# Hybrid decoder step on one core: where v's negated absolute value stands, and how the gate rows are spread over the partitions

## What is computed

```python
proj = h @ w_in
qkv, z, a, b = split(proj)
qkv = silu(causal_conv(qkv, buf, conv_w))      # 4 taps; q, k, v of 128 features each
beta = sigmoid(b)
g = -exp(A_log) * softplus(a + dt_bias)        # one number per token and head
G = cumsum(g)                                  # within a chunk of 128 tokens
decay = exp(G[t] - G[s])
M = eye + strict_lower(beta * (k k^T) * decay)
u, w = M^-1 (v * beta), M^-1 (k * beta * exp(G))
v_new = u - w S;  o = q exp(G) S + (q k^T * decay) v_new
S = exp(G_last) S + (k exp(G_last - G))^T v_new
```

## Time and profile before

| | us |
|---|---|
| median of 3 runs | 1731.76 |
| lowest, highest | 1729.2, 1732.01 |
| the profiled execution | 1732.29 |
| its span, first to last instruction | 1730.5 |
| PE busy / DVE busy / ACT busy | 1664.7 / 1083.1 / 722.5 |
| mean granted TensorE clock | 0.982 of full speed |

### The profile page before, as it was taken

How to read it: one execution, slowest core, us unless ns; L and a number is a source line. 1 busy time by engine, 2 the same in 40 slices (tenths; PEclk the granted TensorE clock), 3 DMA queues, 4 the chain that set the end, 5 groups by cost and what they waited for, 6 DMA issues and landing times.

```text
span 1730.5 us, 33084 instructions
## 1 busy us (share of the span) xinstructions
PE 1664.7 (96%) x12561; PEld 1583.7 (92%) x12561; DVE 1083.1 (63%) x2126; ACT 722.5 (42%) x1315; POOL 35.8 (2%) x85
## 2 busy tenths in 40 slices
PE   6999999999999999999999999999999999999997
PEld 6999999899999999999888888888788999999997
DVE  6898889866435353457778778777846535343443
ACT  6565556534222121225456546655634212222233
POOL 0000000000000000000000000000000000000000
PEclk8999999999999999999999999999998999999998
DMA  6223222222322223222220221122122233222321
GB/s 177 62 83 89 81 81 86 75 74 85 96 86 86 86 86 94 86 74 74 64 64 27 76 64 51 37 67 72 53 62 76 88 93 90 86 85 86 91 79 52
DMA packets 257855, 135.17 MB, mean 78 GB/s; under 512 B 6746, under 2 KB 256180, under 8 KB 257780
## 3 DMA queue, kind: packets, MB, share of 16 engines
q1 hardware_dynamic: 220256, 114.53, 23.0%
q10 hardware_dynamic: 37524, 19.58, 3.9%
HBM read 122.09 MB, written 12.00 MB: 77 GB/s over the span
## 4 chain that ended last, share of the span: by engine, by line
PE 80%; DVE 10%; ACT 5%; issue 3%; ACTq 1%; DMA 0%; DVEq 0%
PE pj L520 66%; PE rr L558 3%; DVE pr L2014 2%; DVE w_lo L1660 1%; PE rr L541 1%; PE rr L633 1%; PE rr L679 1%; PE rr L821 1%; PE rr L837 1%; ACT w_hi L1060 1%; PE rr L748 1%; PE rr L911 1%; PE rr L801 1%; DMA pr<-in_gdn_conv_w_dram 0%; PE rr L917 0%
## 5 line engine op out<-in xcount | busy, mean ns | idle before, releaser
L520 PE MATMUL pj<-xh,w_hi 128*128 128x272 f32 x2064 | 455.7, 302 | 6.6 <-DVE xl L1684 4.7
L1060 ACT ACTIVATE w_hi<-w_raw 128x1024 fp32r<-128x1024 f32 x211 | 222.5, 1055 | 570.0 <-PE pj L520 552.0
L520 PE MATMUL pj<-xh,w_lo 128*128 128x272 f32 x2064 | 431.3, 291 | 0.0
L520 PE MATMUL pj<-xl,w_hi 128*128 128x272 f32 x2064 | 430.1, 290 | 0.0
L520 PEld LDWEIGHTS pj<-xh,w_hi 128*128 128x128 f32 x2064 | 327.0, 191 | 27.2 <-issue 19.6
L520 PEld LDWEIGHTS pj<-xl,w_hi 128*128 128x128 f32 x2064 | 328.7, 191 | 0.0
L520 PEld LDWEIGHTS pj<-xh,w_lo 128*128 128x128 f32 x2064 | 327.0, 191 | 0.0
L1660 DVE TENSOR_TENSOR w_lo<-w_raw,w_hi 128x1024 fp32r<-128x1024 f32 x211 | 256.8, 1217 | 34.0 <-ACT w_hi L1060 33.9
L520 PE MATMUL pj<-oh,w_hi 128*128 128x272 f32 x1254 | 266.7, 294 | 9.1 <-DVE w_lo L1660 6.4
L520 PE MATMUL pj<-oh,w_lo 128*128 128x272 f32 x1254 | 262.1, 291 | 0.0
L520 PE MATMUL pj<-ol,w_hi 128*128 128x272 f32 x1254 | 261.2, 290 | 0.0
(11 more groups left out here) (335 smaller groups left out, 1975.6 us busy)
## 6 DMA issues: line engine op xcount, KB each, us to landing
w_raw<-in_mlp_w_up_dram SPq DMA_DIRECT2D x64, 512.0 KB, 4.0
w_raw<-in_mlp_w_down_dram SPq DMA_DIRECT2D x64, 512.0 KB, 3.6
w_raw<-in_hgrn_w_in_dram SPq DMA_DIRECT2D x32, 512.0 KB, 4.0
w_raw<-in_gdn_w_in_dram SPq DMA_DIRECT2D x32, 512.0 KB, 4.1
out_dram<-S ACTq DMA_DIRECT2D x16, 512.0 KB, 3.2
S<-in_state_hgrn_dram ACTq DMA_DIRECT2D x8, 512.0 KB, 4.0
w_raw<-in_hgrn_w_out_dram SPq DMA_DIRECT2D x8, 512.0 KB, 3.7
S<-in_state_gdn_dram ACTq DMA_DIRECT2D x8, 512.0 KB, 4.1
```

The source lines that it names most:

```text
L520: last = mm(pj[:, s, b, 0:HALF], w[:, s, k, :], v[:, k, b * HALF:(b + 1) * HALF], start=(k == 0 and a == 0), stop=(k == end - 1 and a == 2))
L1060: f(w_hi[:, c % SPLIT, 0:n], w_raw[:, slot, 0:n], ACT.Copy).then_inc(w_high, 1)
```

## The change

It does three things.

- **vneg moves.** DVE makes -|v| of the next head no longer behind the v taps but behind the first chunk's state (L1781), ahead of silu of q; for that it becomes a slot of its own. ACT's slot L6 (exponential and logarithm of it) moves from level 64 to behind the copies of chunk 0, ahead of the square of q. In head 0's own preparation the order is as before.
- **The gate rows are rounded once.** After the gates are made, ACT rounds the lower 64 partitions of `gt4` to fp32r (step `high`, into `gate_parts[0:64]`), and DVE subtracts this from them and rounds the rest into the upper 64 (`low`). Per head DVE no longer makes the 128x544 product but a selector `head_rows` of 128x2 (constant columns, now repeated over the upper half, times the head's column), and PE multiplies `gate_parts` by a selector column in fp32r: one record a matmul where there were two. PE waits once for `low`.
- **gt4 moves** into an unused row of the work space.

```diff
--- before.py
+++ after.py
@@ -75,8 +75,8 @@
     same = s[:, None] // SLEN == s[None, :] // SLEN
     cf[:TS, C_INCLS:C_INCLS + TS] = same & (s[None, :] >= s[:, None])
     cf[:TS, C_NSTRS:C_NSTRS + TS] = -(same & (s[None, :] > s[:, None])).astype(np.float32)
-    cf[0:32, C_IND] = 1
-    cf[32:64, C_IND + 1] = 1
+    cf[:, C_IND] = p // 32 % 2 == 0
+    cf[:, C_IND + 1] = p // 32 % 2 == 1
     cf[:, C_HSEL:C_HSEL + H] = p[:, None] % 32 == np.arange(H)[None, :]
 
     cu = np.zeros((P, 2, len(LEVELS), T // 2), np.uint8)
@@ -159,7 +159,7 @@
         cu = sb("cu", [P, 2 * len(LEVELS) * (T // 2)], U8)
         vec = sb("vec", [P, V_N])
         cw = sb("cw", [P, CONV, 3 * H])
-        hc = sb("hc", [P, 16])
+        hc = sb("hc", [P, 6])
         lbt = sb("lbt", [P, 4, H])
         ones = sb("ones", [P, P])
         epsc = sb("epsc", [P, 2])
@@ -206,7 +206,9 @@
         Sp = sb("Sp", [P, NC, P])
         S0 = sb("S0", [P, NSEQ, P])
 
-        gt4 = sb("gt4", [P, T])
+        gt4 = gd["spare"]
+        gate_parts = sb("gate_parts", [P, T], F32R)
+        head_rows = sb("head_rows", [P, 2], F32R)
         gcol = sb("gcol", [P, NC + 1, 4 * H])
         gnext = sb("gnext", [P, NC + 1])
         gcols = sb("gcols", [P, NC + 1, 4])
@@ -257,10 +259,10 @@
             hr=["d2", "d4", "kl2", "adiag", "kd", "pred1", "d8", "kl4", "pred2", "d16", "kl8", "pred4", "qe",
                 "d32", "kl16", "pred8", "S0", "S1", "S2", "S3", "gate", "d64", "kl32", "pred16", "vbig", "sdec", "kl64", "pred32",
                 "snew", "pred64", "on", "og", "lo"],
-            gp=["x", "neg", "ls", "g", "g2", "scan", "dl", "turn"],
+            gp=["x", "neg", "ls", "g", "g2", "scan", "dl", "turn", "low"],
 
             ga=["cols", "gsel", "k1", "k2", "k3", "kneg", "kls", "q1", "q2", "q3", "qneg", "dec", "ks", "qls",
-                "v1", "v2", "v3", "vneg", "kn", "kb", "qs", "kkd", "vls", "vs", "qn", "zneg", "qkd", "nl", "tt0", "tt1",
+                "v1", "v2", "v3", "kn", "kb", "vneg", "qs", "kkd", "vls", "vs", "qn", "zneg", "qkd", "nl", "tt0", "tt1",
                 "A", "zls", "qe", "cols2", "nbe"],
             ga0=["hcw", "k1", "k2", "k3", "kneg", "cols", "gsel", "kls", "ks", "q1", "dec", "q2", "q3", "qneg", "kn", "kb", "qls", "qs",
                  "kkd", "v1", "v2", "v3", "vneg", "qn", "nl", "tt0", "tt1", "zneg", "qkd", "vls", "vs", "zls", "A",
@@ -279,7 +281,7 @@
             ha=["fabs", "fexp", "fln", "nabs", "cexp", "cln", "qabs", "qexp", "qln", "qsig", "K", "gabs", "gexp", "gln", "e1",
                 "gsig", "ebd"],
             hr=["e2", "e4", "vT", "kdT", "e8", "kdTs", "e16", "e32", "os", "e64", "sq", "oo", "ln", "rn", "hi"],
-            gp=["A", "exp", "ln", "be", "el", "eg", "cols"],
+            gp=["A", "exp", "ln", "be", "el", "high", "eg", "cols"],
             ga=["hist", "past", "ktap", "qtap", "vhist", "kexp", "kln", "G", "ksig", "qexp", "qln", "bb", "dec",
                 "sqk", "vtap", "qsig", "lnk", "rnk", "eG", "vexp", "vln", "sqq", "vsig", "lnq", "rnq", "zexp", "zln", "cout",
                 "K", "tm0", "zsig"],
@@ -725,8 +727,8 @@
                         pe.wait_ge(s.sem, s.after("G" if g else "hist", h))
                     pe.wait_ge(v.sem, v.after("gsel", h))
                     for b in range(2):
-                        last = mm(rr[:, (0 if own else 2) + b, 0:HALF], cf[:, C_IND + g:C_IND + g + 1].broadcast_to([P, P]),
-                                  work[:, b * HALF:(b + 1) * HALF], start=True, stop=True)
+                        last = mm(rr[:, (0 if own else 2) + b, 0:HALF], head_rows[:, g:g + 1].broadcast_to([P, P]),
+                                  gate_parts[:, b * HALF:(b + 1) * HALF], start=True, stop=True)
                     t.did(last, name)
                 if slot == "L5":
                     pe.wait_ge(s.sem, s.after("sqk", h))
@@ -979,6 +981,7 @@
             gdn_pre()
             more(5)
             pe.wait_ge(st["gp"][1].sem, st["gp"][1].after("cols", 0))
+            pe.wait_ge(st["gp"][0].sem, st["gp"][0].after("low", 0))
             gdn_prepare("L3", 0)
             gdn_prepare("L4", 0)
             more(4)
@@ -1268,6 +1271,8 @@
                     last = f(o, i, ACT.Exp)
                 s.did(last, "el")
                 sem_of(v, "turn", 0)
+                sem_of(s, "be", 0)
+                s.did(f(gate_parts[0:64], gt4[0:64], ACT.Copy), "high")
                 s.did(f(gt4[96:96 + H], gt4[0:H], ACT.Exp), "eg")
                 sem_of(t, "cols", 0)
                 f(gcol[:, 0:NC].rearrange("p c (r x) -> p (c r) x", x=H), blocks(rr[:, 2, :], 32)[:, :, 0:H], ACT.Copy)
@@ -1477,8 +1482,6 @@
                         act.wait_ge(st_out, h * 32 + 32 * H)
                         load_state(state_gdn, h)
                     if m == LEVELS[-1]:
-                        if nxt is not None:
-                            gdn_prepare("L6", nxt)
                         break
                     sem_of(t, f"tr{m}", h)
                     if m < LEVELS[-2]:
@@ -1514,6 +1517,8 @@
                                      scale=cf[0:TS, C_SEQ + 4 * c + b:C_SEQ + 4 * c + b + 1])
                         s.did(last, f"vbig{c}")
                     if nxt is not None:
+                        if c == 0:
+                            gdn_prepare("L6", nxt)
                         gdn_prepare(["Q2", "C0", "C2", "C3"][c], nxt)
                     elif c == 2:
                         high(0, U_GOUT + REST)
@@ -1616,7 +1621,7 @@
 
             v, s, t = st["init"]
             nc.vector.memset(epsc[:], EPS).then_inc(unit_out, 2)
-            for buf in (hg["KL"], hg["QL"], hg["A"], gt4[:], gcol[:], dtb[:], xp[:]):
+            for buf in (hg["KL"], hg["QL"], hg["A"], gt4, gcol[:], dtb[:], xp[:]):
                 nc.vector.memset(buf, 0.0)
             after(st["x"][2], "t", 0)
             st["x"][0].did(cp(xT[:, :, 0:P], rr[:, 2:4, :].rearrange("p a (k n) -> p (a k) n", n=P)), "copy")
@@ -2013,7 +2018,7 @@
                             after(v, f"{name}{j - 1}", h)
                         v.did(stt(out=pr[:, row, 0:YW], in0=xp[:, row, j:j + YW], scalar=hcw[:, j, g:g + 1],
                                   in1=pr[:, row, 0:YW], op0=ALU.mult, op1=ALU.add), f"{name}{j}")
-                    if end == CONV:
+                    if end == CONV and name != "v":
                         after(v, f"{name}3", h)
                         v.did(negative_abs(row, YW), f"{name}neg")
 
@@ -2045,7 +2050,7 @@
                     cp(hc[:, 4:5], cf[:, ds(h + C_HSEL, 1)])
                     v.did(cp(gnext[:], of_head(0).rearrange("p c o -> p (c o)")), "cols")
                     after(v, "cols", h)
-                    v.did(ts(work, gt4[:], hc[:, 4:5], None, ALU.mult), "gsel")
+                    v.did(tt(head_rows[:], cf[:, C_IND:C_IND + 2], hc[:, 4:5].broadcast_to([P, 2]), ALU.mult), "gsel")
                 if slot == "W3":
                     low(h * 4, U_GIN + 3)
                 if slot == "L2":
@@ -2076,6 +2081,9 @@
                     low(h * 4, U_GIN + 4)
                 if slot == "L5":
                     convolve("v", "vtap", 0, V_ROW)
+                if slot == "vneg":
+                    after(v, "v3", h)
+                    v.did(negative_abs(0, YW), "vneg")
                 if slot == "L5b":
                     after(s, "rnk", h)
                     after(v, "ks", h)
@@ -2149,6 +2157,8 @@
                 gdn_prepare("L2n", 0)
                 gdn_prepare("L0", 0)
                 after(st["gp"][1], "cols", 0)
+                after(st["gp"][1], "high", 0)
+                st["gp"][0].did(tt(gate_parts[64:128], gt4[0:64], gate_parts[0:64].bitcast(F32), ALU.subtract), "low")
                 gdn_prepare("L1first", 0)
                 gdn_prepare("kls", 0)
                 low(0, U_GIN + 3)
@@ -2163,6 +2173,7 @@
                 gdn_prepare("qs", 0)
                 gdn_prepare("kkd", 0)
                 gdn_prepare("L5", 0)
+                gdn_prepare("vneg", 0)
                 gdn_prepare("q", 0)
                 low(0, U_GIN + 5)
                 gdn_prepare("nl", 0)
@@ -2282,7 +2293,7 @@
                         add_part(U_GOUT, n - 2)
                         low(0, U_GOUT + n)
                 behind_r = {1: ["L6"], 2: ["q", "z", "zneg"], 3: ["W5", "nl"]}
-                behind_S = {0: ["qs"], 1: ["v"], 2: ["qk"], 3: ["inverse"]}
+                behind_S = {0: ["vneg", "qs"], 1: ["v"], 2: ["qk"], 3: ["inverse"]}
                 for c in range(NC):
                     if c:
                         after(t, f"ks{c}", h)
```

## The result

| | before, us | after, us |
|---|---|---|
| median of 10 runs each, measured together | 1730.36 | 1720.09 |
| lowest, highest | 1727.57, 1732.01 | 1719.06, 1725.19 |
| profiled execution | 1732.29 | 1722.71 |
| its span | 1730.5 | 1720.9 |
| mean granted clock | 0.982 | 0.985 |

The ratio is 0.9947, its 95% interval 0.9937 to 0.9958: faster by half a per cent. (The two medians are 10.3 us apart, a quotient of 0.9941, inside that interval.) The forecast was 1725.8 with a low end of 1722.5, so the measured gain was more than the range allowed for. (The three runs known before the prediction had a median of 1731.76 and are among the ten.)

What follows compares the result with a forecast made beforehand. In a head, DVE, then ACT, then DVE were taken to bound until 995.5 us, then PE. The move's 4.7 and head 0's 1.3 made 6.0 us: 1731.76 - 6.0 = 1725.8 us, range 1722.5 to 1730.6.

Steps and rivals of the forecast that it cites:

- rival 2: Gate matmuls in every head: PE's time counts in full, 15.3 us gained in all, 1716.5 us; chance 0.04.
- Part 3: `gsel` made smaller per head, `low` and `high` added once: worth 0, hidden in waits; 1.0 us once if cover failed.
- Rival 1: Behind the first state: cover for -|v| is not enough, only head 0's 1.3 us stay, 1730.4 us; chance 0.12.
- Rival 3: Gate matmuls: fp32r with a broadcast weight costs what fp32 did, head 0 gives nothing, 1727.1 us; chance 0.06.
- Rival 4: In the loop: TensorE's clock falls at the longer pauses, 7 heads cost 11.6 us, 1737.3 us; chance 0.06.
- the term of the move: -|v| leaves the path from v taps to `pred64`: 0.67 us a head, 7 x 0.67 = 4.7 us.
- how the numbers follow: Whole kernel: chances of the outcomes, 0.62 for the forecast, and the range, with one clock window more or less.
- Rival 5: Head 0, at 844 us: the fall to half clock is missed, 1.65 us more gained, 1724.1 us; chance 0.10.

Runs made afterwards that it cites:

- e7: The changed kernel plus one unread DVE instruction of the form of -|v| at the start of the head's preparation, behind `gsel`: 1720.81 us, head periods 58.01 us.
- e9: The changed kernel with -|v| one slot earlier on DVE, right behind `pred64`: 1725.7 us in one run, head periods 58.64 us.
- e2: The kernel before with only the rounded gate rows and the selector, -|v| left in its old place: 1727.69 us, ratio 0.9994.
- e6: The changed kernel plus one unread DVE instruction like -|v| ahead of `os`, with a wait for the third tap's end: 1727.21 us, periods 58.79 us.
- e5: The changed kernel plus one unread DVE instruction like -|v| ahead of `os`, without a wait: 1725.2 us, periods 58.66 us.
- e4: The kernel before, unchanged, in a second profiled execution: 1727.4 us in one run.
- e10: The kernel before, unchanged, in a third profiled execution: 1731.23 us in one run.

## Why the prediction was wrong

**What held.** The gain of the move lies where it was put; the waits became what was forecast (before `vn0` 0.12 for 0.20; before `pred32` 0.94 for 0.94; DVE's idle time behind -|v| 0.75 for 0.7; ACT not waiting for silu of q). Behind `gb` the wait did not grow in one place to 1.1 us: 0.36 stands before `x16` and 0.46 behind it. (Two slips that change nothing: PE also waited 0.47 us for `pred16` at 983.59 before, and 0.46 after, which the prediction doesn't list; and rival 2's sum, 10.7 and 4.7, is 15.4.) Four fp32r matmuls with a broadcast weight took 0.51 us on the chain (forecast 0.49), worth 1.37 us in head 0 (forecast 1.3) and nothing in the loop (forecast 0). Part 3 is hidden as argued: the shown head 0 gained the full 1.37 us with `low` and `high` in it, and e7 shows an instruction longer than `gsel` costing nothing in its place. Rival 1 (cover not enough) is what e9 shows for a place one step off, not for this one. Rival 2 (PE's time counts) falls with e2. Rival 3 falls with the 0.51 us. Rival 4 falls: from `vn0` of head 0 to `vn0` of head 7 the clock stayed at full in all 14 executions, so also behind the pause of 0.94 us that the kernels with the cheaper gate matmuls have in each head.

The Trainium skill (Perfetto Trace Analysis, Identifying the Most-Contended Engine) would have one optimize the most occupied engine first, and judge TensorE by its weight loads' share. Read as less work for that engine, which is how the prediction priced it, the trace does not agree for this loop: the share was 92%, and e2, which takes work from just that engine, leaves the periods at 58.80 us.

**First failing step: the term of the move.** It was sized 0.67 us a head, from the start of -|v| to the start of `os`. It measured 0.79: -|v| also waited some 0.12 us for the third tap to end, a wait that `os` doesn't have (58.79 us in e6, 58.66 in e5). From the taps' start to -|v| were 994.01 - 991.48 = 2.53 us; now `os` follows after 2.42. The prediction took the 2.53 us as fixed and removed only the 0.67 behind them. Over the stages the move gave 0.76 us in head 0 and 4.67 from there to head 7, 5.4 us against 4.7 forecast.

**Second failing step: how the numbers follow.** The range, 1722.5 to 1730.6, was laid around a base taken as exact, with room for one stretch at half clock. The change's own part is 5.4 + 1.4 = 6.8 us where 6.0 was forecast, and this alone would have been in the range, from the old base (1731.76 - 6.8 = 1725.0) and from the new one (1730.36 - 6.8 = 1723.6). The median came out 5.7 us under the forecast: 0.8 by the change's own part, 1.4 by the base, 3.5 by time of no instruction that the change touches.

- The base. 1731.76 was a median of three; ten runs gave 1730.36, 1.4 us less. The text took the three at face value.
- Rival 5, the missed fall at 844, came true in all executions of the changed kernel that were profiled: 1.55 us in the shown pair (36.33 - 34.78). It was priced well (1.65) and given 0.10. But it isn't what the rival said, a pause that moves with the change: the pause is the same, and one execution of the kernel before missed the fall too.
- The stretches that the prediction didn't look at. The end was at half clock in two of three executions of the kernel before and in none of three of the changed one, 1.1 us in the shown pair. The stage ahead of the second MLP gave 0.55 in that pair; e4, the kernel before, has the short value too (50.25), and it goes with where the clock falls behind head 7, so it is not the change's own work.

The runs behind the medians have no trace, so their 3.5 us can't be split by stage. The profiled executions can, three of each kernel. Their spans are 9.4 us apart in the mean (1728.5 and 1719.1): the change's 6.8, then 1.0 for the fall at 844, 0.4 to the second MLP, 0.7 at the end and 0.5 up to the gate columns. The range allowed for one such fall more or less; here there were four such differences, and all came on one side. Whether that is luck stays open.

**What stays open.** Whether the clock falls less often in the changed kernel by its own doing, because its stages stand elsewhere in time, or whether the counts (at 844 two of 3 against none of 11 of all other kernels; at the end two of 3 against none of 3 of the changed one) are chance. Against a simple tie to the time of the pause speak e4 and e10: the same kernel, the pause ending at 842.97 and at 842.89, and only the second falls. The three ratios of the changed kernel, 0.9947, 0.996 and 0.9947, are 9.2, 6.9 and 9.2 us of 1730; the change's own 6.8 us is 0.9961, just outside the interval of the first and inside those of the other two. So some 0 to 2.4 us of what is measured are not the change's own work; by the profiled executions most of them go with the clock.

## What to carry to other kernels

Size a step that is moved off a path from the start of its predecessor to the start of its successor, not by its own length: a wait for the predecessor's result goes with it. Give work on PE no credit where PE waits again before the next point that others wait for, and choose a new place by the idle time right behind it, since one place earlier gave back four fifths of this gain. Compare stage by stage, at full clock on both sides, before a few us are put down to a change, and take a base of few runs with its spread. A stretch at half clock that lies ahead of a wait for another engine costs less than one behind it, so its place counts as well as its presence.

## What the runs showed of the hardware

- A DVE instruction that waits for the end of the one ahead starts 0.12 to 0.13 us later than one that doesn't (128x568, e6 against e5).
- Four fp32r matmuls 128x272 whose weight is one column, broadcast, took 0.51 us in the chain, 0.13 each, close to the 0.123 of those with a full weight; the fp32 ones took 1.83, in eight records.
- The same pause of PE of 1.3 us was followed by 1.2 GHz in two executions of 14, and the one of 2.28 us at the end was followed by work at 1.2 GHz in eight and at 2.4 GHz in six. A pause tells where the clock may fall, not that it will.
- Behind head 7 the clock fell in all 14 executions, at a point that differed by up to 2.4 us, and the stage took 50.24 to 50.28 us where it fell early and 50.60 to 51.02 where it fell late.
